# Stage ends of a two-block transformer kernel: one square moved to VectorE, a high part read twice from PSUM, transposes moved ahead, and a shorter opening

## The reference

```python
# first block (three sublayers), each: normalise, modulate, compute, normalise, gate, add
n = modulate(rmsnorm(h, g_pre[0]), shift(0), scale(0))
h = h + 0.5 * gate(0) * rmsnorm(swiglu(n, ...), g_post[0])              # stage F0
n = modulate(rmsnorm(h, g_pre[1]), shift(1), scale(1))
h = h + gate(1) * rmsnorm(attention_mix(n), g_post[1])                  # stage M1
n = modulate(rmsnorm(h, g_pre[2]), shift(2), scale(2))
h = h + 0.5 * gate(2) * rmsnorm(swiglu(n, ...), g_post[2])              # stage F1
# second block, without the second normalisation
h = modulate_2(rms_norm(x, ffn1_norm), sh1, sc1);  x = x + 0.5 * g1 * swiglu_2(h, ...)   # F2
h = modulate_2(rms_norm(x, mix_norm), sh2, sc2);   x = x + g2 * y                        # M2
h = modulate_2(rms_norm(x, ffn2_norm), sh3, sc3);  x = x + 0.5 * g3 * swiglu_2(h, ...)   # F3
return rms_norm(x, final_norm)
```

## Time and profile before

| | us |
|---|---|
| median of 3 runs (1086.9, 1088.76, 1089.09) | 1088.76 |
| profiled execution, its own time | 1086.96 |
| its span, first to last instruction | 1085.2 |
| TensorE busy in it | 1066.1 (98%) |
| VectorE busy | 853.9 (79%) |
| ScalarE busy | 548.9 (51%) |
| mean granted TensorE clock | 0.997 |

### The profile page before, as it was taken

How to read it: one execution, slowest core, us unless ns; L and a number is a source line. 1 busy time by engine, 2 the same in 40 slices (tenths; PEclk the granted TensorE clock), 3 DMA queues, 4 the chain that set the end, 5 groups by cost and what they waited for, 6 DMA issues and landing times.

```text
span 1085.2 us, 16391 instructions
## 1 busy us (share of the span) xinstructions
PE 1066.1 (98%) x6226; PEld 934.8 (86%) x6226; DVE 853.9 (79%) x939; ACT 548.9 (51%) x669; POOL 48.5 (4%) x78
## 2 busy tenths in 40 slices
PE   7999999999999999999999999999999999999997
PEld 6999999889988788888978888898887778888886
DVE  6889888778887888888778988877876787666665
ACT  4444343564765754444564444445654456444452
POOL 1000000111220100000010000000100000000001
PEclk9999999999999999999999999999999999999999
DMA  9999998467424599997579999844562536666651
GB/s 337 384 405 389 389 402 270 140 160 227 138 79 155 194 343 311 316 319 235 189 248 358 337 367 344 275 171 136 180 209 102 194 117 231 229 215 232 215 175 59
DMA packets 147205, 265.28 MB, mean 244 GB/s; under 512 B 9833, under 2 KB 104534, under 8 KB 142038
## 3 DMA queue, kind: packets, MB, share of 16 engines
q1 hardware_dynamic: 145440, 261.30, 70.1%
q0 software_dynamic: 1056, 3.17, 0.9%
q10 hardware_dynamic: 662, 0.16, 0.1%
HBM read 263.34 MB, written 1.27 MB: 244 GB/s over the span
## 4 chain that ended last, share of the span: by engine, by line
PE 90%; DVE 4%; ACT 2%; issue 1%; POOL 1%; DMA 0%; POOLq 0%; SPq 0%; DVEq 0%; ACTq 0%
PE ps L2021 18%; PE ps L1952 12%; PE ps L1953 11%; PE ps L1954 11%; PE ps L2027 10%; PE ps L2002 7%; PE ps L2004 6%; PE ps L2005 6%; PE ps L2178 1%; PE ps L2256 1%; ACT w_hi L851 1%; PE ps L2551 1%; DVE x_res L1422 1%; PE ps L2161 1%; DVE nT L1268 1%
## 5 line engine op out<-in xcount | busy, mean ns | idle before, releaser
L851 ACT ACTIVATE w_hi<-w_raw 128x2048 fp32r<-128x2048 f32 (+3 forms) x172 | 317.9, 1854 | 255.3 <-PE ps L1954 93.6
L1245 DVE TENSOR_TENSOR w_lo<-w_raw,w_hi 128x2048 fp32r<-128x2048 f32 (+1 forms) x160 | 360.3, 2254 | 101.3 <-ACT w_hi L851 100.4
L2021 PE MATMUL ps<-nT_both,w_hi 128*128 128x512 f32 x864 | 210.8, 391 | 0.0
L2021 PEld LDWEIGHTS ps<-nT_both,w_hi 128*128 128x128 f32 x864 | 158.8, 188 | 30.7
L2002 PE MATMUL ps<-nT_both,w_hi 128*128 128x256 f32 x576 | 164.8, 286 | 0.0
L2005 PE MATMUL ps<-nT_both,w_lo 128*128 128x256 f32 x576 | 163.1, 283 | 0.0
L2004 PE MATMUL ps<-nT_both,w_hi 128*128 128x256 f32 x576 | 163.1, 283 | 0.0
L1337 DVE SCALAR_TENSOR_TENSOR arena<-arena,c_act 128x3072 f32<-128x3072 f32 (+2 forms) x49 | 129.4, 2651 | 0.0
L1952 PE MATMUL ps<-w_hi,hT_hi 128*128 128x512 f32 x320 | 125.1, 391 | 0.0
L1953 PE MATMUL ps<-w_lo,hT_hi 128*128 128x512 f32 x320 | 125.1, 391 | 0.0
L1954 PE MATMUL ps<-w_hi,hT_lo 128*128 128x512 f32 x320 | 124.6, 389 | 0.0
(11 more groups left out here) (326 smaller groups left out, 1269.1 us busy)
## 6 DMA issues: line engine op xcount, KB each, us to landing
arena<-in_w_ada SPq DMA_DIRECT2D x16, 1536.0 KB, 10.7
arena<-in_ada_w SPq DMA_DIRECT2D x16, 1536.0 KB, 8.3
w_raw<-in_w_in SPq DMA_DIRECT2D x44, 512.0 KB, 4.6
w_raw<-in_ffn_w_down SPq DMA_DIRECT2D x44, 512.0 KB, 4.1
w_raw<-in_w_ffn_down SPq DMA_DIRECT2D x42, 512.0 KB, 4.8
w_raw<-in_ffn_w_gate SPq DMA_DIRECT2D x42, 512.0 KB, 4.2
w_raw<-in_ffn_w_up SPq DMA_DIRECT2D x42, 512.0 KB, 5.1
w_raw<-in_w_ffn_gate SPq DMA_DIRECT2D x41, 512.0 KB, 6.9
```

The lines of the kernel that those rows point to most:

```text
L851: copy = lambda o, i: act.activation(o, i, ACT.Copy)
L1245: dve.tensor_tensor(lo(s, n), raw(s, n), hi(s, n).bitcast(F32), ALU.subtract).then_inc(lo_ready[s], 1)
L2021: pe.matmul(ps[:, i, :], hi(s)[:, cols], nT_both[:, 4 * half + k].rearrange("p a n -> p (a n)"), start=(half == 0 and k == 0), stop=False, ...
```

## The change

All six stages keep their order and their arithmetic, apart from the parts below.

1. After F0, F1, F2 and M2 (`ON_BOTH`), tile 0's square is shared: ScalarE squares an added column and the first 511 columns, VectorE squares the last 513 with ScalarE's sum as its start. The added column of `x_and_eps` holds sqrt(epsilon * 1024), so GpSimd only takes the power.
2. Pair 0 of tile 0 is transposed twice (`turned_twice`), at all five ends: once into bank 1, from which ScalarE writes `nT_hi` with two Identity activations, and once into the usual bank, from which VectorE makes both blocks of `nT`. VectorE waits for pair 1's transposes, since only one of the two turns counts.
3. After F0, F1 and F2 (`NEXT_B`) the high part of the next weight piece is made in 512 and 1536 columns, the first ahead of the last hidden part, and its whole low part stands ahead of the gating. After M2 the rest of the low part follows the new square.
4. After F0, M1 and F1, ScalarE squares tile 1's first output half ahead of VectorE's gating of it, which now waits for that; the order was the other way round.
5. After F2 and M2 (`TURNED_EARLY`) tile 0's transposes stand ahead of the last three products of the stage before.
6. In the opening, row 3 of half 1 goes from TensorE to VectorE, the last row on TensorE comes after column step 12 instead of 9, and the five spins before F0 are gone.

```diff
-        ON_DVE = [[0, 1, 2, 3, 4, 5, 6], [0, 1, 4, 5, 6]]
-        ON_PE = [[7], [2, 3, 7]]
+        ON_DVE = [[0, 1, 2, 3, 4, 5, 6], [0, 1, 3, 4, 5, 6]]
+        ON_PE = [[7], [2, 7]]
+        TURNED_EARLY = ["M2", "F3"]
+        NEXT_B = ["F0", "F1", "F2"]
-        ON_ACT = [(0, 0, 0), (0, 1, 0), (0, 1, 1), (1, 0, 0), (1, 0, 1), (1, 1, 0), (1, 1, 1)]
+        ON_ACT = [(0, 1, 0), (0, 1, 1), (1, 0, 0), (1, 0, 1), (1, 1, 0), (1, 1, 1)]
+        ON_BOTH = [(f, 0) for f in ("M1", "F2", "M2", "F3")]
+        def turned_twice(f, t, pair):
+            return f != "F0" and (t, pair) == (0, 0)
+        def second_at(i):
+            return ps[:, 1, i * P:(i + 1) * P]
...
+                if (f, t) in ON_BOTH:                                   # GpSimd, norm_rms
+                    pool.wait_ge(sq_done, squares(f, t))
+                    pool.tensor_tensor(stat[:, 8:9], stat[:, 2:3], minus_half[:, 0:1], ALU.pow).then_inc(rms_done, 1)
...
+                if (f, t) in ON_BOTH:                                   # ScalarE, norm_square
+                    act.wait_ge(h_half, 2 * NORM[f] - 1)
+                    act.activation(y_row[:, 0, 0:NB], x_and_eps[:, 0, 7:NB + 7], ACT.Square, scale=D ** -0.5,
+                                   accum_out=stat[:, 0:1]).then_inc(sq_done, 1)
+                    return
...
+                    if turned_twice(f, t, j):                           # ScalarE, norm_hi
+                        act.wait_ge(n_tr, pair_count(f, t, j))
+                        for k in range(2):
+                            last = act.activation(nT_hi[:, k, cols], second_at(k), ACT.Identity,
+                                                  scale=mod_col[:, NORM[f], 0, k:k + 1], bias=mod_col[:, NORM[f], 1, k:k + 1])
+                        last.then_inc(n_hi, 1)
+                        continue
...
-                    if t and n == 0:                                    # ScalarE, output_squares
-                        act.wait_ge(gated_first, STAGES.index(stage) + 1)
-                    else:
-                        output_ready(act, stage, t, n)
+                    output_ready(act, stage, t, n)
+                    if t and n:
+                        act.wait_ge(gated_first, STAGES.index(stage) + 1)
...
-                dve.wait_ge(n_tr, pair_count(f, t, pair))               # VectorE, norm_cols
+                dve.wait_ge(n_tr, pair_count(f, t, pair + 1 if turned_twice(f, t, pair) else pair))
...
-                if stage in POST and (t, n) != (1, 0):                  # VectorE, gated
+                if stage in POST:
                     dve.wait_ge(fsq_done, 4 * POST[stage] + 2 * t + n + 1)
...
+                if stage in NEXT_B:                                     # VectorE, boundary
+                    s, use = next_b
+                    dve.wait_ge(first_hi, len(OPENERS) + NEXT_B.index(stage) + 1)
+                    dve.tensor_tensor(lo(s)[:, 0:HI_CUT], raw(s)[:, 0:HI_CUT], hi(s)[:, 0:HI_CUT].bitcast(F32), ALU.subtract)
+                    dve.wait_ge(hi_ready[s], use + 1)
+                    lo_rest(s, HI_CUT)
+                elif next_b:
                     lo_begin(*next_b, LO_CUT)
                 residual(stage)
-                if next_b:
+                if stage == "M1":
+                    lo_rest(next_b[0], LO_CUT)
+                if (f, 0) in ON_BOTH:
+                    rest = slice(NB - 1, D)
+                    dve.wait_ge(sq_done, squares(f, 0) - 1)
+                    dve.wait_ge(h_done, 2 * NORM[f] - 1)
+                    dve.tensor_tensor_reduce(out=y_row[:, 1, rest], in0=x_res[:, 0, rest], in1=x_res[:, 0, rest], op0=ALU.mult,
+                                             op1=ALU.add, scale=1.0 / D, scalar=stat[:, 0:1], accum_out=stat[:, 2:3]).then_inc(sq_done, 1)
+                if stage == "M2":
                     lo_rest(next_b[0], LO_CUT)
                 if f != "end":
+                    if (f, 0) in ON_BOTH:
+                        dve.wait_ge(sq_done, squares(f, 0))
                     gated(stage, 1, 0).then_inc(gated_first, 1)
...
+                    if turned_twice(f, t, pair):                        # TensorE, norm_transposes
+                        for k in range(2):
+                            last = pe.transpose(second_at(k), y_row[:, 0, k * P:(k + 1) * P], ident[:])
+                        last.then_inc(n_tr, 1)
...
+                            if turn and n and is_last and j == 1:       # TensorE, last_tile of F2
+                                turn()
...
-                    for _ in range(2 if i < 6 else 1):                  # TensorE, row_sums
-                        next(early, None)
-                    if i == 9:
+                    next(early, None)
+                    if i == 12:
...
-            spin(5)
             ffn("F0")
...
+                    if t and n:                                         # TensorE, the output product of M2
+                        row_group(s, banks[n], NB, None, 4, tiles=(t,), ks=range(3))
+                        norm_transposes("F3", 0)
+                        row_group(s, banks[n], NB, None, 4, stop=True, tiles=(t,), ks=[3]).then_inc(w_used[s], 1)
+                        continue
```

More of the change, by code:

```diff
@@ L24 @@
 LO_CUT = 1408
+HI_CUT = 512
 OUT_CUT = 704
@@ L56, in sem @@
             return ctx.enter_context(nc.semaphore(name))
-        x_res = sb("x_res", [P, T, D])
+        x_and_eps = sb("x_and_eps", [P, T, D + 8])
+        x_res = x_and_eps[:, :, 8:D + 8]
         y_row = sb("y_row", [P, T, D])
@@ L424, in norm_at @@
         def norm_at(f, t, pair, i):
-            if f != "F0" and (t, pair, i) == (0, 0, 1):
-                return ps[:, 1, 0:P]
             at = (2 * (pair % 2) if f == "F0" else 0) + i
             return ps[:, norm_bank(f, t, pair), at * P:(at + 1) * P]
+        def turned_twice(f, t, pair):
+            return f != "F0" and (t, pair) == (0, 0)
+        def second_at(i):
+            return ps[:, 1, i * P:(i + 1) * P]
         def wait(e, s, v):
@@ L762, in _ @@
             pool.memset(minus_half[:], -0.5).then_inc(pool_step, 1)
-            pool.wait_ge(pool_step, 2)
+            pool.memset(x_and_eps[:, 0, 7:8], (EPS * D) ** 0.5).then_inc(pool_step, 1)
+            pool.wait_ge(pool_step, 3)
             pool.affine_select(out=ident[:], in_=ones[:], compare_op=ALU.is_equal, fill=0.0, base=0,
@@ L775, in rms @@
                     pool.tensor_scalar(ss, ss, more, EPS, ALU.add, ALU.add).then_inc(pool_step, 1)
-                pool.wait_ge(pool_step, 3 + len(made))
+                adds.append(name)
+                pool.wait_ge(pool_step, 3 + len(adds))
                 pool.tensor_tensor(dst, ss, minus_half[:, 0:dst.shape[1]], ALU.pow).then_inc(rms_done, 1)
@@ L967, in ffn @@
                 body(f, NC - 1, extra=next_e and (*next_e, n))
+                if next_b:
+                    s, use = next_b
+                    act.wait_ge(raw_loaded[s], use * 32 + 32)
+                    act.wait_ge(w_used[s], use)
+                    copy(hi(s)[:, 0:HI_CUT], raw(s)[:, 0:HI_CUT]).then_inc(first_hi, 1)
                 act.wait_ge(h_ready, NC * (FFN.index(f) + 1))
@@ L971, in ffn @@
                 if next_b:
-                    split_hi(*next_b, n)
+                    copy(hi(s)[:, HI_CUT:PIECE], raw(s)[:, HI_CUT:PIECE]).then_inc(hi_ready[s], 1)
             def load_c(i):
@@ L1274, in norm_lo @@
                 dve.wait_ge(n_hi, pair_count(f, t, pair))
+                if turned_twice(f, t, pair):
+                    cols_ready(dve, f, t, pair)
                 dve.tensor_tensor(nT_lo[:, k, c], nT[:, k, c], nT_hi[:, k, c].bitcast(F32), ALU.subtract).then_inc(n_lo, 1)
@@ L1972, in norm_transposes @@
                         last = pe.transpose(norm_at(f, t, pair, i), y_row[:, t, k * P:(k + 1) * P], ident[:])
-                    last.then_inc(n_tr, 1)
+                    if not turned_twice(f, t, pair):
+                        last.then_inc(n_tr, 1)
             def norm_waits(first_norm, tiles, kk):
@@ L2066, in downs, with last_downs @@
                 last.then_inc(w_used[s], 1)
-            def last_downs(f):
+            def last_downs(f, turn=None):
                 i = FFN.index(f) * NC
@@ L2073, in last_downs @@
                     if t:
-                        last_tile(((s0, use0), (s1, use1)))
+                        last_tile(((s0, use0), (s1, use1)), turn)
                         return
@@ L2087, in last_downs, with last_tile @@
                         last.then_inc(out_bank, 1)
-            def last_tile(pieces):
+            def last_tile(pieces, turn):
                 for n in range(2):
@@ L2116, in first_rows @@
                 for t in range(T):
-                    if t == 0:
+                    if t == 0 and f not in TURNED_EARLY:
                         norm_transposes(f, t)
@@ L2249, in ffn @@
                 body(f, NC - 1, first=lambda: sum_folds(f))
-                last_downs(f)
```

(1 more changed line is left out.)

8 lines of the change are left out of this document (5 added, 3 removed).

## The result

Measured side by side, the changed kernel takes 1090.97 us against 1087.14 of the kernel before: ratio 1.0033, 95% interval 1.0024 to 1.0042. It is **slower by 3.8 us**, 0.33%, beyond the prediction's own border of 0.2%; it had given 0.36 to slower and 0.50 to no change. One execution of after and one of e8_kept_busy took over twice as long as the others (2134 and 2453 us) and stay out of the ratios; without its own, e8's median is 1089.84. The three runs of before that the prediction started from had a median of 1088.76; the later medians of the same kernel lie at 1086.9 to 1087.1, so the start of the sum was 1.6 to 1.9 us too high. The predicted 1090.4 is near the measured time by luck: this and a sum 2.1 us too small cancel.

What follows compares the result with a forecast made beforehand. The prediction took TensorE, with matmuls in 98% of the span, as the bound, its stage-end waits hanging mainly on VectorE. Ends +2.2 and opening -0.5 gave +1.7: 1088.76 + 1.7 = 1090.4 us, range 1086.5 to 1092.6.

Steps and rivals of the forecast that it cites:

- The bound: TensorE has matmuls in 98% of the span; its waits at stage ends were said to hang mainly on VectorE.
- the ends: Five stage ends: +0.52 us after F0, +0.96 M1, +0.52 F1, +0.08 F2, +0.08 M2, together +2.2.
- An operation added there is paid in full: At a stage end, any operation added on VectorE between the row's scaling and pair 2's blocks costs its full time.
- The low part ahead of gating, at nothing: After F0, F1 and F2, the moved low part fits into existing ScalarE and VectorE waits and costs nothing.
- The opening: Before and early in F0: half 1's products start earlier, -0.5 us, bounds -0.6 and +0.3.
- The working of the queue: In the opening, VectorE goes on at 38.04 instead of 38.57, and half 1's products start that much before 41.08.
- Rival 1: Opening: without the spins the clock stays low as long again, half 1 starts 0.25 later; 1091.2 us, chance 30%.
- the clock row at 24 us: In the opening, the clock shown at 24 us was to tell the forecast from Rival 1.
- the forecast: Whole kernel: ends +2.2 and opening -0.5 give +1.7, 1090.4 us, chance 36%.
- Rival 2: Stage ends: VectorE's wait for pair 1 does not bind, ends -1.6, opening -0.5; 1086.6 us, chance 14%.
- Rival 3: Stage ends: extra block and wait overlap, each end near nothing, leaving -0.5; 1088.3 us, chance 20%.
- The base: Starting time of the sum for the whole kernel before: median 1088.76 us, the profiled execution's own time being 1086.96.

Runs made afterwards that it cites:

- e8_kept_busy: e3 plus 22 matmuls by a weight of zeros in three of TensorE's waits in the opening: 1089.97 us.
- e1: The changed kernel with the whole opening of the kernel before, so only the stage ends changed: 1089.18 us.
- e5: e1 with pair 0 transposed once and its first column block made by ScalarE as before: 1086.96 us.
- e3: The changed kernel with only the five useless matmuls ahead of the first products put back: 1090.72 us.
- e4: The changed kernel with row 3 of half 1 and the spread of the sums as before, without the five useless matmuls: 1089.56 us.
- e2: The kernel before with the changed opening alone, all stage ends as before: 1088.74 us.
- e7: e1 with pair 0's two sets of transposes swapped, VectorE's first; VectorE waits for that alone, ScalarE for pair 1's: 1087.78 us.
- e6: e5 with VectorE gating tile 1's first half after F0, M1 and F1 without waiting for ScalarE's square: 1086.69 us.
- e10: e1 with tile 0's transposes after F2 and M2 put back behind the last products: 1090.87 us.
- e9: e6 with the changed opening, the five useless matmuls and 18 matmuls by zeros in two of TensorE's waits: 1087.11 us.

## Why the prediction was right or wrong

**The bound and the ends: right.** "An operation added there is paid in full": the second block's 0.32 (0.73 less 0.41) and the 0.53 of waiting, less what the end gained ahead of them, came through to pair 2 within 0.1 us at each end. Term by term after F0: scaling at 217.05 foreseen, 217.07 measured; wait 0.47 foreseen, 0.53 measured; the gating later by 0.52, measured 0.59. M1: scaling 360.74 foreseen, 360.70 measured. F2: VectorE's first block at 735.66 foreseen, 739.57 - 3.92 = 735.65 measured. The sum of the ends was 2.16 foreseen and 2.2 measured, and e1 gives 2.3 for them alone.

**The low part ahead of gating, at nothing: not contradicted.** No row behind it is late in e5, whose ends hold it too and come to -0.3.

**The opening: wrong, the step that failed.** The prediction put half 1's start 0.5 earlier and then said "nothing else holds these products ... so the gain stays". The working of the queue was sound: in e3, VectorE goes on at 38.11 (38.04 foreseen) and half 1 starts at 40.62, 0.46 earlier than before. In after all of it ran later, the second set of 24 useless matmuls at 14.95 instead of 14.43 already, so that 0.11 was left of it. But the speed of the products was taken from before. The clock stands in the prediction only at 24 us, where a row showed it low, and not at 41, behind the sixteen one-column matmuls that the change puts between waits (0.41 and 0.28 idle in the rows above). Twelve products at 0.43 instead of 0.23 took back the gain and 1.9 more. Why the clock fell there stays open; that it falls there more often with the row moved is what the profiles and times of e1 and e3 speak for.

**Rival 1: its mechanism is there, and it is not what decided.** That the clock stays low as long again without the useless matmuls is seen in the profiles of e4 (20.6 to 27.4) and e2 (18.9 to 25.7). Its total, +2.45, fell short of the +3.8 by the fall over half 1, which no rival held. In after's own profile the clock did not even fall at 20.5, so there the whole loss is half 1's, and the sign that I had named, the clock row at 24 us, would have spoken for the forecast.

**Rival 2: it did not happen,** the wait binds. But e5 shows that its price was wrong too: with that wait and block gone the ends gave -0.3, not -1.6, since ScalarE's square of the last product and TensorE's last product are late next. I had said what is late next for costs and not for gains.

**Rival 3: the parts do not cancel;** nothing of block and wait overlaps.

**The base.** A median of three, with runs of 1088.76 and 1089.09 among them, was taken as the kernel's time though the profiled execution had 1086.96. In the comparison beside e5 to e8, 24 of 31 executions of before lie from 1086.7 to 1087.5 at a mean clock of 0.997 or 0.998, and seven from 1089.0 to 1091.8 at 0.992 to 0.995: the median of three probably rests on two such low-clock executions. From 1087.1 the same terms give 1088.8, some 2.1 below the measured time, and that is how far the prediction was off.

## What to carry to other kernels

Before an engine's work is thinned out, ask what its clock will do in the dense work right behind: here taking one row of sums off TensorE cost 1.5 us by the medians, with half 1's products at half clock in all three profiles of it without filling. When two consumers need copies made by one engine, give the first place, and the first count, to the consumer on the path: e7 moved two sets of transposes past each other and saved 1.4 us. Work out for a gain too what is late next; a step that comes 0.26 earlier gives nothing if the wait behind it hangs on something else.

## What the runs showed of the hardware

- **The same opening meets the low clock at different places.** With before's opening the clock was at half from 20.5 to 23.9 in before, 19.8 to 23.2 in e1, 38.4 to 41.8 in e7 and 37.5 to 44.3 in e6; in e10 both early and late. The times show it too: the 31 executions of before fall into 24 and seven, as above, and e2's ten runs lie in two groups, four from 1087.6 to 1087.8 and six from 1088.5 to 1089.3. The Trainium skill (TensorE: Matmul & The Clock Gate, Part 1: The HAM clock gate) says that the chip watches TensorE's activity in a window that runs freely and does not start anew with a kernel. These runs agree: one profiled execution is one draw, and a stretch of thin work is a risk with a share, not a fixed cost.
- **Waits alone don't explain it.** With row 3 on TensorE the engine was hardly idle ahead of half 1 (0.31 in before); it had 18 one-column matmuls there, and the clock still fell during or right behind them in e6, e7 and e10, three of seven such profiles. With the row moved and the waits open it fell in after, e2 and e3, all three, at 39.2 to 39.5, ahead of the long wait in after and e2 and 0.3 into it in e3; with the waits filled, in the profiles of e8 and e9, in neither, though e8's other executions have lower means. That is few draws, and which of the one-column matmuls and the waits weighs more was not told apart.
- **What TensorE does in the low stretch went with how long it lasted**: about 3.4 us in before, e1, e5, e9 and e10, where useless matmuls stood in it, and 6.8 in e2 and e4, early in the opening without them. The late stretches don't fall into that order: 3.4 in e7, 6.8 in after, e3, e6 and e10.
